# Positional scores on the two row halves, and two weight tiles ahead of the modulation tiles, in a fused transformer kernel

## The reference

```python
def swiglu(h, w_in, w_out):            # first block, two layers, hidden width 2816
    g, u = jnp.split(h @ w_in, 2, axis=-1)
    return (jax.nn.silu(g) * u) @ w_out

# last attention: 16 heads, q_nope/k_nope 128 wide, q_pe/k_pe 64 wide, v 128 wide
q_a, kv_a, k_pe, z = jnp.split(h_lat @ w_in, splits, axis=-1)
q_nope, q_pe = queries(q_a)                       # rmsnorm, then w_qb, per head
q_pe = _apply_rope(q_pe, ...); k_pe = _apply_rope(k_pe, ...)   # k_pe is one for all heads
k_nope, v = keys_values(kv_a)                     # rmsnorm, then w_kvb, per head
s = q_nope @ k_nope.T + q_pe @ k_pe.T             # 512 queries x 768 keys
p = softmax(s * MLA_SCALE); o = p @ v
y = (o * silu(z)) @ w_out
```

## Time and profile before

| | |
|---|---|
| median of 3 runs | 4166.31 us (4159.05 to 4175.61) |
| the profiled execution | 4176.91 us, of which its span is 4175.1 |
| mean granted clock of TensorE | 0.949 of full speed |
| PE, DVE, ACT, POOL busy | 91%, 39%, 25%, 13% of the span |
| first feed-forward, in | about 530 to 970 us |
| second feed-forward, in | about 1533 to 1860 us |
| last attention, heads | about 3446 to 4044 us |

### The profile page before, as it was taken

How to read it: one execution, slowest core, us unless ns; L and a number is a source line. 1 busy time by engine, 2 the same in 40 slices (tenths; PEclk the granted TensorE clock), 3 DMA queues, 4 the chain that set the end, 5 groups by cost and what they waited for, 6 DMA issues and landing times.

```text
span 4175.1 us, 50272 instructions
## 1 busy us (share of the span) xinstructions
PE 3789.1 (91%) x19826; PEld 2648.6 (63%) x19826; DVE 1629.6 (39%) x2525; ACT 1059.0 (25%) x1554; POOL 533.0 (13%) x252
## 2 busy tenths in 40 slices
PE   6888999999978889899899999999968979999998
PEld 4565588875556647764688888888855544444443
DVE  4544300000056520000377878788881132222211
ACT  4333111110023411110233333333310023333320
POOL 2220144420122025540000000000000000000000
PEclk9888999999989999999899999999989979999999
DMA  5221233332111133442111111111121101001002
GB/s 223 70 85 70 91 118 118 116 126 66 55 46 31 41 128 131 153 151 85 68 49 45 49 40 54 44 43 36 41 81 35 46 25 31 30 25 30 29 26 65
DMA packets 81446, 292.00 MB, mean 70 GB/s; under 512 B 8224, under 2 KB 10272, under 8 KB 80416
## 3 DMA queue, kind: packets, MB, share of 16 engines
q1 hardware_dynamic: 75632, 274.30, 19.5%
q10 hardware_dynamic: 5680, 15.73, 1.0%
HBM read 275.32 MB, written 14.68 MB: 69 GB/s over the span
## 4 chain that ended last, share of the span: by engine, by line
PE 42%; issue 33%; DVE 7%; POOLq 6%; POOL 5%; DVEq 3%; ACT 2%; DMA 1%; ACTq 0%; SPq 0%
PE ps L447 14%; PE ps L462 11%; POOLq L412 6%; POOL ringA_r L413 4%; PE ps L1015 3%; PE ps L1013 2%; PE ps L1047 2%; DVEq L1807 2%; PE ps L823 1%; PE ps L881 1%; DVE rstd L1882 1%; DVE arena L1806 1%; PE ps L493 1%; PE ps L892 1%; PE ps L1024 1%
## 5 line engine op out<-in xcount | busy, mean ns | idle before, releaser
L462 PE MATMUL ps<-x_r,ringB_r 128*128 128x512 f32 (+1 forms) x2704 | 945.7, 350 | 39.0 <-POOL ringA_r L413 26.0
L462 PE MATMUL ps<-x_r,ringA_r 128*128 128x512 f32 (+1 forms) x2704 | 956.5, 354 | 18.5 <-ACT arena L1348 13.1
L447 PE MATMUL ps<-arena,ringA 128*128 128x512 f32 (+1 forms) x2208 | 796.4, 524 | 21.8 <-DVEq L1911 9.4
L447 PEld LDWEIGHTS ps<-arena,ringA 128*128 128x128 f32 x2208 | 421.1, 191 | 396.7 <-issue 377.5
L462 PEld LDWEIGHTS ps<-x_r,ringB_r 128*128 128x128 f32 x2704 | 514.4, 190 | 124.6 <-POOL ringA_r L413 30.2
L462 PEld LDWEIGHTS ps<-x_r,ringA_r 128*128 128x128 f32 x2704 | 514.9, 190 | 103.6 <-issue 27.2
L462 PE MATMUL ps<-a_r,ringA_r 128*128 128x512 f32 x1600 | 542.2, 339 | 0.0
L462 PE MATMUL ps<-a_r,ringB_r 128*128 128x512 f32 x1104 | 400.8, 363 | 0.0
L411 POOL TENSOR_TENSOR ringB_r<-ringA,consts 128x1024 fp32r<-128x1024 f32 x104 | 197.6, 1900 | 1031.6 <-DMA ringA<-streamA 1031.6
L462 PEld LDWEIGHTS ps<-a_r,ringA_r 128*128 128x128 f32 x1600 | 302.5, 189 | 34.6 <-issue 1.0
L1625 DVE TENSOR_TENSOR arena<-arena,ps 128x768 f32 (+1 forms) x44 | 36.1, 821 | 667.5 <-ACT arena L1193 386.1
(11 more groups left out here) (255 smaller groups left out, 4841.5 us busy)
## 6 DMA issues: line engine op xcount, KB each, us to landing
ringA<-streamA SPq DMA_DIRECT2D x236, 512.0 KB, 3.6
arena<-streamC SPq DMA_DIRECT2D x136, 512.0 KB, 5.5
ringB<-streamB SPq DMA_DIRECT2D x100, 512.0 KB, 3.6
x<-x_in SPq DMA_DIRECT2D x2, 3072.0 KB, 12.0
x_scratch<-x ACTq DMA_DIRECT2D x6, 1024.0 KB, 5.2
a<-streamC SPq DMA_DIRECT2D x8, 512.0 KB, 11.9
x<-x_scratch SPq DMA_DIRECT2D x2, 2048.0 KB, 8.6
x_scratch<-x ACTq DMA_DIRECT2D x2, 1536.0 KB, 8.3
```

The costliest lines, as they stand in the source:

```text
L447: mm = nc.tensor.matmul(ps[0:m, bank + half, 0:tn], ring[:, slot, w0 + k * P:w0 + k * P + m], src[:, k0 + k, t0:t0 + tn], start=start and ...
L462: mm = nc.tensor.matmul(ps[:, bank + half, 0:tn], wk, src[:, k, t], start=k == 0 and i == 0, stop=k == DC - 1 and i == 2)
```

## The change

In the last attention, `scores` takes two query blocks. It runs the 128-wide products of both, and then their positional products alternately: the first block's on rows 0 to 63 of the array into banks 0 and 1, the second block's on rows 64 to 127 into banks 2 and 3. For that `kpe`, the positional queries `qp`, the rotation matrix and the cos/sin tables are held twice, on partitions 0 to 63 and 64 to 127; the weights of kpe and qp are laid out twice, in room that the stream had unused. The order of PE, ACT and DVE in a head follows. The second pair of blocks waits for both exponentials of the first. Every tensor keeps its place and the bytes loaded stay the same.

In the feed-forwards, SP issues slots 0 and 1 of a round, then the four C tiles, then slots 2 and 3.

```diff
                 with sp.Fori(0, n) as g:
-                    load_C(g + 12 * (l + 1))
                     for s in range(RA):
+                        if s == 2:
+                            load_C(g + 12 * (l + 1))
                         load_A(g + first, s)
...
-                    product(ringA, s, a, 2 * s - 2, T, m=HEAD if s == 3 else P).then_inc(readA, 1)
+                    product(ringA, s, a, 2 * s - 2, T).then_inc(readA, 1)
...
-                            mm = nc.tensor.matmul(ps[0:HEAD, 7, :], W[:, 256 + k * HEAD:256 + (k + 1) * HEAD], M["qa"][:, k, :],
+                            mm = nc.tensor.matmul(ps[:, 7, :], W[:, 640 + k * P:640 + (k + 1) * P], M["qa"][:, k, :],
                                                   start=k == 0, stop=k == 1)
...
-                    def scores(u):
-                        b = 2 * (u % 2)
-                        if u == 0:
+                    def scores(first):
+                        if first == 0:
                             pe.wait_ge(sem("ml_rope"), h + 1)
                             pe.wait_ge(sem("ml_kc"), h + 1)
-                        if u >= 2:
-                            pe.wait_ge(sem("ml_exp"), h * 4 + u - 1)
+                        else:
+                            pe.wait_ge(sem("ml_exp"), h * 4 + 2)
+                        for j in range(2):
+                            for t0, tn, half in pieces(T):
+                                nc.tensor.matmul(ps[:, 2 * j + half, 0:tn], B["qn"][:, (first + j) * P:(first + j + 1) * P],
+                                                 B["kn"][:, t0:t0 + tn], start=True, stop=False, skip_group_check=True)
                         for t0, tn, half in pieces(T):
-                            nc.tensor.matmul(ps[:, b + half, 0:tn], B["qn"][:, u * P:(u + 1) * P], B["kn"][:, t0:t0 + tn],
-                                             start=True, stop=False)
-                            mm = nc.tensor.matmul(ps[:, b + half, 0:tn], B["qp"][0:HEAD, u * P:(u + 1) * P],
-                                                  M["kpe"][0:HEAD, t0:t0 + tn], start=False, stop=True)
-                        mm.then_inc(sem("ml_sc"), 1)
+                            for j in range(2):
+                                r = slice(j * HEAD, (j + 1) * HEAD)
+                                mm = nc.tensor.matmul(ps[:, 2 * j + half, 0:tn], B["qp"][r, (first + j) * P:(first + j + 1) * P],
+                                                      M["kpe"][r, t0:t0 + tn], start=False, stop=True, skip_group_check=True)
+                        mm.then_inc(sem("ml_sc"), 2)
...
                     scores(0)
-                    scores(1)
                     nxt("z")
+                    scores(2)
                     turn(0)
-                    scores(2)
                     nxt("qn", "qp")
                     turn(1)
-                    scores(3)
                     nxt("rot", "kl")
...
-                nc.scalar.activation(M["kpe"][0:HEAD, :], psf[0:HEAD, 2048:2048 + T], ACT.Copy).then_inc(sem("ml_low"), 1)
+                nc.scalar.activation(M["kpe"], psf[:, 2048:2048 + T], ACT.Copy).then_inc(sem("ml_low"), 1)
...
                     exps(2)
                     nxt("qn", "qp")
+                    exps(3)
                     copy_p(1)
-                    exps(3)
                     nxt("kl")
...
                     maxima(0)
                     maxima(1)
                     normalise(0)
+                    normalise(1)
                     maxima(2)
-                    normalise(1)
+                    maxima(3)
                     normalise(2)
-                    maxima(3)
+                    normalise(3)
                     if follow:
                         rope_q(h + 1, 1 - e)
-                    normalise(3)
```

More of the change, by code:

```diff
@@ L1419, in evacuate @@
                     what = dict(z=(B["z"], ps[:, 7, :], ACT.Silu), qn=(B["qn"], ps[:, 6, :], ACT.Copy),
-                                qp=(B["qp"][0:HEAD, :], ps[0:HEAD, 7, :], ACT.Copy), kl=(B["kn"][:, 0:LAT], ps[:, 7, :], ACT.Copy),
+                                qp=(B["qp"], ps[:, 7, :], ACT.Copy), kl=(B["kn"][:, 0:LAT], ps[:, 7, :], ACT.Copy),
                                 kc=(B["kn"][:, LAT:T], ps[:, 6, 0:CTX], ACT.Copy), vl=(v[:, 0:LAT], ps[:, 7, :], ACT.Copy),
@@ L1914, in mla @@
             def mla():
-                cos, sin = C("cos64")[0:HEAD, :], C("sin64")[0:HEAD, :]
+                cos, sin = C("cos64"), C("sin64")
                 dve.wait_ge(sem("ml_lowms"), 1)
@@ L1918, in mla @@
                 TS(M["rk"], psf[:, 1024:1024 + T], 1.0 / P, EPS, ALU.mult, ALU.add)
-                rope(M["kpe"][0:HEAD, 0:LAT], ps[0:HEAD, 4, :], M["tmp"][0:HEAD, :], cos, sin)
+                rope(M["kpe"][:, 0:LAT], ps[:, 4, :], M["tmp"], cos, sin)
                 dve.drain()
-                TT(M["kpe"][0:HEAD, 0:LAT], M["kpe"][0:HEAD, 0:LAT], M["tmp"][0:HEAD, :], ALU.add)
+                TT(M["kpe"][:, 0:LAT], M["kpe"][:, 0:LAT], M["tmp"], ALU.add)
                 nc.vector.reciprocal(M["rq"], M["rq"])
@@ L1931, in rope_q @@
                 def rope_q(h, e):
-                    q = MP[e]["qp"][0:HEAD, :]
+                    q = MP[e]["qp"]
                     dve.wait_ge(sem("ml_rot"), h + 1)
-                    rope(q, ps[0:HEAD, 6, :], M["tmp"][0:HEAD, :], cos, sin)
+                    rope(q, ps[:, 6, :], M["tmp"], cos, sin)
                     dve.drain()
-                    TT(q, q, M["tmp"][0:HEAD, :], ALU.add).then_inc(sem("ml_rope"), 1)
+                    TT(q, q, M["tmp"], ALU.add).then_inc(sem("ml_rope"), 1)
                 def step(g, e, follow):
@@ L2053, in make_consts @@
         if m < 32:
-            rot[m + 32, m] = -1
+            rot[m + 32, [m, m + HEAD]] = -1
         else:
-            rot[m - 32, m] = 1
+            rot[m - 32, [m, m + HEAD]] = 1
     put("rot64", rot)
@@ L2064, in make_consts @@
     put("sin128", np.sin(ang))
-    d = np.arange(HEAD) % 32
+    d = np.arange(P) % 32
     ang = pos[d // 16] * inv[d % 16][:, None]
@@ L2141 @@
     w = i["mla_w_in_2"][0]
-    low = np.concatenate([tiles(np, w[:, 0:256]), tiles(np, w[:, 256:384]), tiles(np, w[:, 384:448])])
+    low = np.concatenate([tiles(np, w[:, 0:256]), tiles(np, w[:, 256:384]), tiles(np, np.concatenate([w[:, 384:448]] * 2, axis=1))])
     qb = i["mla_w_qb_2"][0].reshape(2, P, HEADS, 192)
@@ L2147 @@
         wb[:, :, k * P:(k + 1) * P] = qb[k, :, :, 0:P].transpose(1, 0, 2)
-        wb[:, :, 256 + k * HEAD:256 + (k + 1) * HEAD] = qb[k, :, :, P:].transpose(1, 0, 2)
+        for at in (0, HEAD):
+            wb[:, :, 640 + k * P + at:640 + k * P + at + HEAD] = qb[k, :, :, P:].transpose(1, 0, 2)
     wb[:, :, 384:640] = kvb.transpose(1, 0, 2)
```

## The result

The changed kernel takes 4059.45 us (median of four runs, 4053.36 to 4063.39) against 4168.2 us for the kernel before beside it (4159.05 to 4175.61): a ratio of 0.9739, with a 95% interval of 0.9715 to 0.9763. The forecast was 4059, with 4036 to 4100 as its range. The profiled execution took 4053.36 us with a span of 4051.6, which is 123.5 us less than the span before.

The account below looks back on a forecast made before the run. PE was taken to bound the attention heads, and PE's waits for POOL to cost the second feed-forward time and clock. Gains of 61 + 5 + 41 = 107 us take the median from 4166.31 to 4059, range 4036 to 4100.

Parts of the forecast that it names:

- Rival 2: Last attention: pairs overlap, but DVE's and ACT's chain ends 2.6 us a head later; 4100; chance 0.17 together with Rival 1.
- Rival 1: Last attention: row halves do not overlap when adding to a begun bank; 4100; chance 0.17 together with Rival 2.
- The walk through the new order: Last attention: PE, ACT and DVE followed through one head; 37.3 to 33.3 us, fifteen heads gaining 61 us.
- the sum: Whole kernel: gains of 61 (fifteen heads), 5 (last head) and 41 us (second feed-forward), together 107 us.
- The new wait: Last attention: second pair waits for the first's exponentials; costs nothing while z covers it, 3.4 us without.
- The last head: Last attention's final head, with no z to hide behind: 32 or 33 us against 37.63; gain 5, bounds 2 and 9.
- Rival 3: Second feed-forward: first weight tile still lands late, no gain there; 4100; chance 0.10, including any feed-forward gain under 26.
- The term of 41 us: Second feed-forward, ten rounds: 292.0 to 250.9 us, PE's stalls and the slow clock both gone; 26 if slow stretches stay.
- The C tiles are covered: Second feed-forward: C tiles issued some 3 us later, but PE reads them over 15 us on, so no cost.
- Rival 4: Last attention: three stalls a head bring the clock to 0.73, head 44.7 us; 4236; chance 0.07 with anything like it.
- The Trainium skill's warning: Last attention: emptying PSUM may limit; by that rule the overlap's 2.6 us a head is lost, total gain 68 us.

Follow-up runs that it names:

- same_half: Changed kernel, but both positional products of a pair run on rows 0 to 63, so the halves do not overlap; 4097.55 us, ratio 0.984.
- no_cover: Changed kernel, but PE issues the second pair of score blocks ahead of z, straight behind the first pair; 4145.8 us, ratio 0.9947.
- one_ahead: Changed kernel, but only the first weight tile of a round is issued ahead of the C tiles, the second behind them; 4080.34 us, ratio 0.9795.
- c_last: Changed kernel, but the four C tiles are issued behind all four weight tiles of a round; 4073.8 us, ratio 0.9781.
- pairs_only: Changed kernel's new attention with the old order of loads, C tiles ahead of the weight tiles; 4093.18 us, ratio 0.9834.

## Why the prediction was right, point by point

- **PE bounds a head, and what its program loses is time.** Shown: `same_half` gives back 2.56 us a head, exactly what its passes take longer. Rival 2, the chain on ACT and DVE, is out with it.
- **A pair of row halves takes 1.5 us, also when it adds to a begun bank.** Shown: 1.49 us. Rival 1 (4100) is out; the kernel that has its condition by construction took 4097.55.
- **The walk through the new order.** I had 33.3 us for a head, it is 33.01. The waits before kc and the values were 1.25 and 0.9 us by my walk and are 1.08 and 0.82. The third, 0.3 us before the rotation, is not in the profile as a wait: from turn(1) to the rotation it is 0.91 us, where the other turns take 0.65 to 0.71 to the next product. These 0.2 us can be the change to 64 rows or the end of ACT's copies at 3580.71; the runs don't tell them apart. Fifteen heads give 65.0 us where the sum has 61.
- **The new wait is free under z and costs 3.4 us without.** Shown by `no_cover`: 3.45 us.
- **The last head** gives 6.9 us, the sum has 5, within 2 to 9.
- **Weight tiles land in order of issue, so two of them ahead of the C tiles take the stall out.** Shown: landing in 3.6 us, no wait of PE for POOL in ten rounds, and `one_ahead` shows that the second tile is needed too. Rival 3 is out.
- **The clock comes back with the stall.** The term of 41 us measured 44.1 by the two profiles. PE's work in a round is 24.8 us where I took 25.09 from a round that still had its stall in it. The 0.3 us are an effect of how the profile counts around a stall: back to back these passes start every 0.23 us, but the last one ahead of the stall counts with its whole 0.39, and from the first one behind it to the next it is 0.34 us (1801.83 to 1802.17), together 0.27.
- **The C tiles are covered.** Shown in the change, though against the moment when the first weight slot is free they are issued 4.0 us later than before (1.3 us after it in place of 2.7 ahead), where I had some 3; and `c_last` shows where the cover ends: issued some 12 us later they make PE wait 1.5 us a round. Their slack is about 10 us: in the change the last one is issued at 1597.0 and lands at 1604.7, and PE reads them at 1614.4.
- **Rival 4, the clock in the heads.** It did not happen: 1.00 in a head, with stalls of 1.08 and 0.82 us. But it is real: in `no_cover` it happens, and the kernel is then nearly as slow as before (0.9947). One reading in its support was too simple: the stall of 2.74 us lies in the round of the earlier trace rows whose clock is 1.00, and 0.94 is the mean over rounds that differ; the last section comes back to this.

The sum was 107 us against a measured 108.8. It hits better than its terms do: by the two profiles they come to 65.0, 6.9 and 44.1, together 116.0, so by the profiles each term was too small. That 4059 met 4059.45 is partly luck: the kernel before was itself 1.9 us slower in this comparison than in the 4166.31 I started from, and the interval on the ratio is about 10 us wide either way. The part of the 44.1 that is clock varies, as `pairs_only` shows with 286.2 in place of 292.0 us for the old order, and its two profiles' difference of 38.3 us would make it 110. The Trainium skill's warning (TensorEngine Tiling (Array Packing), PSUM Bottleneck) does not decide here: ACT is busy for 14.38 us and DVE for 9.99 in a head of 33.01, and the overlap came through in full.

## What to carry to other kernels

Products with half of the array's rows in use are worth pairing even where they only add to a bank: here it took 1.28 us out of every 2.77. Group the passes of one shape as well, and look for something long to put between the pair and the wait that it makes, since the uncovered gap cost more than itself through the clock. In a queue of loads, put first what another engine still has to work on, and check how long the things that slide back can wait. When an order is rewritten, walk every engine's queue once, for a small operation may have slid behind one that it needn't wait for: rope behind a division cost 0.64 us a head.

## What the runs showed of the hardware

I had not expected the same stall to cost so differently. By whole stretches the granted clock goes down as the gap that recurs in each round of the second feed-forward gets longer: it is 1.00 with 1.5 us a round (`c_last`), 0.98 with 2.3 (`one_ahead`, 22.6 us over ten) and 0.94 or 0.96 with 2.6 (the kernel before and `pairs_only`, 26.0 and 26.3 over ten). Single rounds do not follow the length. These are three rounds of the kernel before, in the columns of rows 2; the gaps in them are 1.97, 2.83 and 2.91 us.

```profile
1580.38:1609.04 28.66, 26.69 (x138) 20.84 (x137) 1.45 (x3) 4.37 (x6) 16.97 (x8) 0.94 0.42 147
1669.21:1699.93 30.72, 27.89 (x138) 21.74 (x137) 1.45 (x3) 4.36 (x6) 16.94 (x8) 0.89 0.40 137
1758.09:1786.08 27.99, 25.08 (x138) 19.70 (x137) 1.45 (x3) 4.36 (x6) 16.95 (x8) 1.00 0.43 146
```

The shortest of the three gaps goes with 0.94 and the longest with 1.00. Eight of the ten rounds of the kernel before are below 1.00 and four of the ten of `pairs_only`; in `one_ahead` it is the first three (0.94), while the rest have 1.00 with gaps of 1.9 to 2.3 us. So how long the gap is does not alone decide whether the clock falls; what else does, no run here shows. No round of `c_last` fell, with gaps of up to 1.95 us.

In the heads, which run other passes and are only compared with each other, waits of 1.08 and 0.82 us go with 1.00 and 3.45 us with 0.94, and there the clock took another 2.3 us a head. The fall sits right behind the gap: in `no_cover` the clock is 0.62 over the 4.47 us from 3565.99, in which eight passes take 4.54 us in place of 2.74, and 1.00 over the 33.5 us that follow. The Trainium skill, TensorE: Matmul & The Clock Gate, HAM oscillation — how this bites in real kernels, describes this pattern of a wait in every loop after which the next matmuls start slow; the rows agree with the pattern. The waits of its example are of 3 to 5 us, and here waits of 2 to 3 us were already enough in some rounds.
